# A mixture-of-experts loop: an expert's slot list made first in the program of the expert two places ahead

## The chip, the cores and the metric

The kernel runs on one core of a Trainium2 chip. The metric is the device time of one execution in microseconds (us). A core has five engines with programs of their own, which meet only at semaphores: TensorE (PE in the profile, PEld for its weight loads), VectorE (DVE), ScalarE (ACT), GpSimd (POOL) and SyncE (SP), the last of which here only starts transfers.

## The reference

The reference is a small decoder trunk in float32: 512 tokens of 1024 features, two layers. Layer 0 mixes tokens with a short gated convolution, layer 1 with sparse attention. After the mixer each layer has a mixture of 16 experts with a shared router:

```python
for e in range(N_EXPERTS):
    gate, up = jnp.split(tok @ w_gu[e], 2, axis=-1)
    out = out + comb[:, e:e + 1] * ((jax.nn.silu(gate) * up) @ w_down[e])
```

`comb` is zero except for the two experts that the router picks for a token, so an expert needs only its own tokens. `w_gu[e]` is 1024 x 1024 and `w_down[e]` is 512 x 1024, so 6 MB of weights are read for each expert. Around the mixtures stand modulation, residuals and layer norms.

## The kernel before, in words

Products are done in split form for accuracy. Every float32 operand x is written as hi + lo: ScalarE copies it to a rounded hi, VectorE subtracts to get lo, and TensorE does three matmuls (lo·hi, hi·lo, hi·hi; `mm3`, lines 203 to 205) where one would do. Weights come in blocks of 1 MB (128 x 2048 float32). For each block SyncE starts the load (`load_part`, line 916), ScalarE writes `w_hi` (`step_hi`, line 934), VectorE writes `w_lo` (`step_lo`, line 941), and TensorE does 12 matmuls of 128x512. There are six raw buffers, in which `w_lo` overwrites the raw block, and three of `w_hi`. TensorE counts used blocks in the semaphore `blk_used`, and `step_hi` of block b waits until block b - 3 is used:

```python
act.wait_ge(blk_used, b - NSPLIT + 1)        # line 938, NSPLIT = 3
```

An expert has six blocks. In the program of expert e (`expert_pe`, line 961), TensorE does blocks 0 and 1 (the second half of its own gate and up product), blocks 2 and 3 (the first half of expert e + 1's), and blocks 4 and 5 (e's `w_down`). Between block 0 and block 1 it transposes the gathered token rows of expert e + 1 (`rows_pe`, line 879, eight transposes into banks 6 and 7). ScalarE and VectorE turn these into `xe_hi` and `xe_lo` (`rows_act`, `rows_dve`). After block 2 TensorE makes the slot list of expert e + 2 and then transposes `hh`, the silu(gate)·up of expert e, which VectorE makes from ScalarE's `sg` (lines 999 and 1027).

The slot list says which token sits in which of an expert's 128 slots. Three steps make it:

- `one_hot` (line 850), VectorE: compares slot numbers with the tokens' positions, into `oneh`, of which there are two buffers. It is the first instruction of VectorE's program for expert e, for expert e + 2.
- `list_pe` (line 857), TensorE: four bf16 matmuls with two columns of output into bank 7. It waits for the one-hot (`oh_made`) and until the list before it was read (`tok_made`).
- `list_dve` (line 866), VectorE: adds the two columns into `tok`.

GpSimd waits for `tok` and starts an indirect transfer (`gather`, line 871) that fetches the 128 token rows to `xg`, two buffers. Its rows are used one program later, by `rows_pe` in the program of expert e + 1.

The order on each engine is written out by hand and is fixed. Before VectorE comes to the program of an expert it has made `w_lo` of that expert's blocks 0, 1 and 2, in the tail of the program before (line 1035, i from 5 to 8); ScalarE has made their `w_hi` in the same way (line 1005). Programs of two experts, with p = 0 and 1, form a pair; the first pair and the last are unrolled and the six between are a loop (`all_experts`, line 1052). The last pair's programs make no list.

Of the kernel before, what the change touches and what calls it, by code (L numbers as in the profile page):

```python
# [49 lines left out]
def hybrid_trunk(nc, x, c, ada_w, ada_b, ln_g, ln_b, conv_w_in, conv_w, conv_b, conv_w_out,  # L50
# [27 lines left out]
    with ExitStack() as ctx:  # L78
# [122 lines left out]
        def mm3(o, lh, ll, rh, rl, start, stop):  # L201

            nc.tensor.matmul(o, lh, rl, start=start, stop=False)  # L203
            nc.tensor.matmul(o, ll, rh, start=False, stop=False)  # L204
            return nc.tensor.matmul(o, lh, rh, start=False, stop=stop)  # L205
# [438 lines left out]
        PAIRS = NE // 2  # L644
# [75 lines left out]
        def bc(ap, shape, axis):  # L720

            return ap.unsqueeze(axis).to_broadcast(shape)
# [121 lines left out]
        def after(eng, semaphore, value):  # L844
            if not isinstance(value, int) or value > 0:
                if isinstance(semaphore, Count):
                    semaphore, value = semaphore.at(value)
                eng.wait_ge(semaphore, value)

        def one_hot(dve, s, pair, p):  # L850

            after(dve, s.tok_mm, 2 * pair + p - 1)
            shape = [P, TT, P]
            nc.vector.tensor_tensor(oneh[:, p, :, :], bc(slots[:], shape, 1),
                                    bc(posm[:, 2 * pair + p, :], shape, 2), ALU.is_equal).then_inc(s.oh_made.sem, 1)

        def list_pe(pe, s, pair, p):

            pe.wait_ge(*s.oh_made.at(2 * pair + p + 1))
            after(pe, s.tok_made, 2 * pair + p)  # L860
            for i in range(TT):
                m = nc.tensor.matmul(bank[7][:, 0:2], oneh[:, p, i, :], tokc[:, i, :], start=(i == 0),
                                     stop=(i == TT - 1))
            m.then_inc(s.tok_mm.sem, 1)

        def list_dve(dve, s, pair, p):
            dve.wait_ge(*s.tok_mm.at(2 * pair + p + 1))
            after(dve, s.xg_in[p], 16 * pair)
            nc.vector.tensor_scalar(tok[:, p, :], bank[7][:, 0:1], bank[7][:, 1:2], None, ALU.add).then_inc(s.tok_made.sem, 1)  # L869
# [6 lines left out]
                                    in_offset=bass.IndirectOffsetOnAxis(ap=tok[:, p, :], axis=0)  # L876
                                    ).then_inc(s.xg_in[p].sem, 16)

        def rows_pe(pe, s, pair, p):

            pe.wait_ge(*s.xg_in[p].at(16 * pair + 16))
            after(pe, s.xe_lo_made, 2 * pair + p)
            after(pe, s.ht_lo_made, 2 * pair + p - 1)
            pe.wait_ge(*s.tok_made.at(2 * pair + p + 1))
            for k in range(KD):
                m = nc.tensor.transpose(bank[6 + k // 4][:, (k % 4) * P:(k % 4 + 1) * P],  # L886
                                        xg[:, p, k * P:(k + 1) * P], ident[:])
            m.then_inc(s.xg_turned.sem, 1)
# [10 lines left out]
        def rows_dve(dve, s, pair, p):  # L899
            dve.wait_ge(*s.xe_hi_made.at(2 * pair + p + 1))  # L900
            for h in range(2):
                m = nc.vector.tensor_tensor(xe_lo[:, p, 4 * h:4 * h + 4, :],  # L902
                                            bank[6 + h][:].rearrange("p (k t) -> p k t", k=4),
                                            xe_hi[:, p, 4 * h:4 * h + 4, :].bitcast(F32), ALU.subtract)
            m.then_inc(s.xe_lo_made.sem, 1)
# [4 lines left out]
        def step_block(s, pair, p, i):  # L910

            first = s.b0 + 2 + EBLK * p + i
            return (first + 2 * EBLK * pair, first % NRAW, first // NRAW + 2 * EBLK // NRAW * pair,
                    first % NSPLIT)
# [26 lines left out]
        def step_lo(dve, s, pair, p, i):  # L941
            b, slot, _, hslot = step_block(s, pair, p, i)
            if not isinstance(b, int) or b < B_END:
                dve.wait_ge(hi_done, b + 1)
                nc.vector.tensor_tensor(w_lo[:, slot, :], raw[:, slot, :], w_hi[:, hslot, :].bitcast(F32),  # L945
                                        ALU.subtract).then_inc(lo_done, 1)

        def gate_up(pe, s, pair, p, i, q, j):

            b, slot, _, hslot = step_block(s, pair, p, i)  # L950
            pe.wait_ge(lo_done, b + 1)
            for kk in range(2):
                k = 2 * j + kk
                for h in range(2):
                    c_ = slice(kk * D + h * FF, kk * D + (h + 1) * FF)
                    m = mm3(bank[2 * q + h][:], xe_hi[:, q, k, :], xe_lo[:, q, k, :], w_hi[:, hslot, c_],
                            w_lo[:, slot, c_], start=(k == 0), stop=(k == KD - 1))
            m.then_inc(blk_used, 1)


        def expert_pe(pe, s, pair, p, last=False):
            e, q = 2 * pair + p, 1 - p
            gate_up(pe, s, pair, p, 0, p, 2)
            if not last:
                rows_pe(pe, s, pair + p, q)
            gate_up(pe, s, pair, p, 1, p, 3)
            if not last:
                pe.wait_ge(*s.xe_lo_made.at(e + 2))
                after(pe, s.h_made, e)
                gate_up(pe, s, pair, p, 2, q, 0)  # L970
            if not (isinstance(pair, int) and pair == PAIRS - 1):
                list_pe(pe, s, pair + 1, p)
            pe.wait_ge(*s.h_made.at(e + 1))
            for k in range(4):
                m = nc.tensor.transpose(bank[6][:, k * P:(k + 1) * P], hh[:, k * P:(k + 1) * P], ident[:])
            m.then_inc(s.h_turned.sem, 1)
            if not last:
                gate_up(pe, s, pair, p, 3, q, 1)
            pe.wait_ge(*s.ht_lo_made.at(e + 1))
            after(pe, s.y_made, e)  # L980
            for j in range(2):
                b, slot, _, hslot = step_block(s, pair, p, j + (2 if last else 4))
                pe.wait_ge(lo_done, b + 1)
                for kk in range(2):
                    k = 2 * j + kk
                    for h in range(2):
                        c_ = slice(kk * D + h * BANK, kk * D + (h + 1) * BANK)
                        m = mm3(bank[4 + h][:], ht_hi[:, k, :], ht_lo[:, k, :], w_hi[:, hslot, c_], w_lo[:, slot, c_],
                                start=(k == 0), stop=(k == 3))
                m.then_inc(blk_used, 1)  # L990
# [27 lines left out]
        def expert_dve(dve, s, pair, p, last=False):  # L1018
            e = 2 * pair + p
            if not (isinstance(pair, int) and pair == PAIRS - 1):  # L1020
                one_hot(dve, s, pair + 1, p)
            if not last:
                rows_dve(dve, s, pair + p, 1 - p)
            step_lo(dve, s, pair, p, 3)
            dve.wait_ge(*s.sg_made.at(e + 1))
            after(dve, s.h_turned, e)
            nc.vector.tensor_tensor(hh[:], sg[:], bank[2 * p + 1][:], ALU.mult).then_inc(s.h_made.sem, 1)  # L1027
            if not last:
                step_lo(dve, s, pair, p, 4)
            dve.wait_ge(*s.ht_hi_made.at(e + 1))  # L1030
            nc.vector.tensor_tensor(ht_lo[:], bank[6][:].rearrange("p (k t) -> p k t", k=4),  # L1031
                                    ht_hi[:].bitcast(F32), ALU.subtract).then_inc(s.ht_lo_made.sem, 1)
            if not (isinstance(pair, int) and pair == PAIRS - 1):
                list_dve(dve, s, pair + 1, p)
            for i in range(5, 9) if not last else range(4, 7):
                step_lo(dve, s, pair, p, i)


        def begin_pe(pe, s):
            pe.wait_ge(*s.xe_lo_made.at(1))  # L1040
            gate_up(pe, s, 0, 0, -2, 0, 0)
            gate_up(pe, s, 0, 0, -1, 0, 1)
# [200 lines left out]
        def moe_dve(dve, s):  # L1243
# [15 lines left out]
            rows_dve(dve, s, 0, 0)  # L1259
            begin_dve(dve, s)  # L1260
            all_experts(dve, expert_dve, s)
            over_dve(dve, s)
            for i in range(TT + 1):
# [19 lines left out]
        def moe_pe(pe, s):  # L1283
            for i in range(TT):
                turn_pe(pe, s.turn, us[:, i % 2, :], i)
            router_pe(pe, s)
            places_pe(pe, s)
            list_pe(pe, s, 0, 0)
            list_pe(pe, s, 0, 1)
            pe.wait_ge(*s.turn.lo.at(2 * TT))  # L1290
            pe.wait_ge(*s.tok_made.at(2))
            rows_pe(pe, s, 0, 0)
            begin_pe(pe, s)
            all_experts(pe, expert_pe, s)
            over_pe(pe, s)
# [873 lines left out]
```

## Time and profile before

| | |
|---|---|
| median of 3 runs | 1640.94 us (1638.69 to 1645.2) |
| profiled execution, its own time | 1636.06 us |
| its span, first to last instruction | 1634.3 us |
| TensorE / VectorE / ScalarE / GpSimd busy | 1293.1 / 1111.3 / 761.9 / 188.4 us |
| granted TensorE clock, mean | 0.888 |
| experts of layer 0 / of layer 1 | about 355 to 671 us / 1270 to 1579 us |

Times inside the trace count from the start of the span. "Busy" adds up the instructions' durations; matmuls overlap, so their starts tell more than their durations. The granted clock is 1.00 at 2.4 GHz and 0.50 at 1.2 GHz. In the timeline, a bracket behind an instruction gives how long its engine had been idle before it and which instruction, on which engine, ended that.

### The profile page before, as it was taken

To read this page: it belongs to the slowest core of one execution; us is meant where nothing else is said; L and a number is where in the kernel's file an instruction comes from. 1 tells how busy PE (TensorE), PEld (TensorE's weight loads), DVE (VectorE), ACT (ScalarE), POOL (GpSimd) and SP (SyncE) were. 2 spreads that over 40 slices of the span, in tenths; PEclk is the share of its full clock that TensorE was granted. 3 is DMA by queue.
4 is the path that set the end of the run, shared out by engine and by line. 5 is a ranking of instruction groups with operands and counts; after the bars stand their busy time and mean duration, and the time that the engine had idled before them with its cause. 6 is when DMAs were issued, how large, how long until landed. Compare 5 with 4: busy or idle time off the path is not lost. (4 is left out here: it accounts for less than half of the span.)

```text
span 1634.3 us, 18079 instructions
## 1 busy us (share of the span) xinstructions
PE 1293.1 (79%) x6537; PEld 1025.4 (63%) x6537; DVE 1111.3 (68%) x1210; ACT 761.9 (47%) x836; POOL 188.4 (12%) x257
## 2 busy tenths in 40 slices
PE   1499968349999999339768999999933999999950
PEld 0377747137777777238766788887822777777730
DVE  5568665648889888475644556555375699898846
ACT  0223212217777777423322444446121677777732
POOL 2011110200000000120000112111030000000012
PEclk9899989569999999659957999999965999999975
DMA  8467763229999999722401222231421799999942
GB/s 304 186 233 243 247 228 118 92 79 351 380 364 389 388 392 389 274 77 80 131 5 52 91 78 91 81 120 41 161 98 69 271 381 393 390 394 387 396 180 87
DMA packets 107407, 356.01 MB, mean 218 GB/s; under 512 B 7746, under 2 KB 16062, under 8 KB 107342
## 3 DMA queue, kind: packets, MB, share of 16 engines
q1 hardware_dynamic: 82920, 268.47, 43.7%
q0 software_dynamic: 19568, 69.78, 12.3%
q10 hardware_dynamic: 4854, 16.88, 2.5%
q8 instruction: 42, 0.69, 0.2%
q14 instruction: 23, 0.19, 0.0%
HBM read 329.89 MB, written 25.21 MB: 217 GB/s over the span
## 5 line engine op out<-in xcount | busy, mean ns | idle before, releaser
L945 DVE TENSOR_TENSOR w_lo<-raw,w_hi 128x2048 fp32r<-128x2048 f32 x189 | 433.4, 2298 | 86.9 <-ACT w_hi L939 86.8
L939 ACT ACTIVATE w_hi<-raw 128x2048 fp32r<-128x2048 f32 x189 | 362.4, 1918 | 89.5 <-PE bank L205 74.5
L203 PE MATMUL bank<-w_lo,xe_hi 128*128 128x512 f32 x512 | 212.8, 416 | 7.6 <-DVE xe_lo L902 7.3
L204 PE MATMUL bank<-w_hi,xe_lo 128*128 128x512 f32 x512 | 204.6, 400 | 0.0
L205 PE MATMUL bank<-w_hi,xe_hi 128*128 128x512 f32 x512 | 204.3, 399 | 0.0
L198 DVE TENSOR_TENSOR w_lo<-raw,w_hi 128x2048 fp32r<-128x2048 f32 x37 | 84.9, 2300 | 150.1 <-ACT w_hi L193 149.6
L193 ACT ACTIVATE w_hi<-raw 128x2048 fp32r<-128x2048 f32 x37 | 70.4, 1908 | 155.0 <-PE bank L205 154.3
L203 PE MATMUL bank<-u_lo,w_hi 128*128 128x512 f32 x320 | 134.1, 419 | 7.0 <-DVE q L1619 3.6
L205 PE MATMUL bank<-u_hi,w_hi 128*128 128x512 f32 x320 | 128.9, 403 | 0.0
L204 PE MATMUL bank<-u_hi,w_lo 128*128 128x512 f32 x320 | 128.8, 403 | 0.0
L318 DVE SCALAR_TENSOR_TENSOR acc<-ada,silu_c,acc 128x1024 f32<-128x1024 f32 x88 | 112.4, 1277 | 12.4 <-DMA ada<-in_ada_w_dram 7.7
L203 PEld LDWEIGHTS bank<-w_lo,xe_hi 128*128 128x128 f32 x512 | 97.7, 191 | 36.9 <-issue 10.8
L1855 ACT ACTIVATE prob<-bank,snm 128x512 f32<-128x512 f32 (+3 forms) x128 | 62.3, 525 | 117.2 <-DVE snm L1914 94.1
L205 PEld LDWEIGHTS bank<-w_hi,xe_hi 128*128 128x128 f32 x512 | 97.7, 191 | 23.7
L204 PEld LDWEIGHTS bank<-w_hi,xe_lo 128*128 128x128 f32 x512 | 98.0, 191 | 19.4
L203 PE MATMUL bank<-w_lo,ht_hi 128*128 128x512 f32 x256 | 103.5, 404 | 4.9 <-DVE ht_lo L1031 4.2
L358 PE MATMUL bank<-ident,us 128*128 128x128 f32 x128 | 30.4, 416 | 95.1 <-DVE us L389 95.1
L875 POOL DMA_INDIRECT xg<-scratch_u,tok x32 | 33.8, 1055 | 604.9 <-DVE tok L869 604.3
L204 PE MATMUL bank<-w_hi,ht_lo 128*128 128x512 f32 x256 | 102.5, 401 | 0.0
L205 PE MATMUL bank<-w_hi,ht_hi 128*128 128x512 f32 x256 | 102.4, 400 | 0.0
L1914 DVE TENSOR_REDUCE snm<-bank 128x1 f32<-128x384 f32 (+1 forms) x96 | 46.2, 509 | 64.3 <-PE bank L1708 64.1
L358 PEld LDWEIGHTS bank<-ident,us 128*128 128x128 f32 x128 | 24.4, 218 | 102.5 <-DVE us L389 77.5
(255 smaller groups left out, 2439.1 us busy)
## 6 DMA issues: line engine op xcount, KB each, us to landing
raw<-in_w_gu_dram SPq DMA_DIRECT2D x128, 1024.0 KB, 7.9
raw<-in_w_down_dram SPq DMA_DIRECT2D x64, 1024.0 KB, 8.3
ada<-in_ada_w_dram POOLq DMA_DIRECT2D x64, 512.0 KB, 5.6
scratch_y<-ye ACTq DMA_DIRECT2D x32, 512.0 KB, 7.4
ada<-in_ada_w_dram SPq DMA_DIRECT2D x32, 512.0 KB, 3.7
raw<-in_conv_w_in_dram SPq DMA_DIRECT2D x12, 1024.0 KB, 10.2
rows<-scratch_mods POOLq DMA_DIRECT2D x12, 512.0 KB, 5.0
raw<-in_w_kv_dram SPq DMA_DIRECT2D x6, 1024.0 KB, 9.1
```

The source lines that it names most:

```text
L193: nc.scalar.activation(w_hi[:, b % NSPLIT, :], raw[:, b % NRAW, :], ACT.Copy).then_inc(hi_done, 1)
L198: nc.vector.tensor_tensor(w_lo[:, s, :], raw[:, s, :], w_hi[:, b % NSPLIT, :].bitcast(F32), ALU.subtract).then_inc(lo_done, 1)
L203: nc.tensor.matmul(o, lh, rl, start=start, stop=False)
L204: nc.tensor.matmul(o, ll, rh, start=False, stop=False)
L205: return nc.tensor.matmul(o, lh, rh, start=False, stop=stop)
L318: nc.vector.scalar_tensor_tensor(out=a, in0=s.ring[:, t % s.n_ring, :], scalar=silu_c[:, k:k + 1], in1=a if k or s.bias is None else s.bia ...
L358: t = nc.tensor.transpose(bank[4 + n % 4][:, q * P:(q + 1) * P], src[:, (4 * h + q) * P:(4 * h + q + 1) * P], ident[:])
L875: pool.indirect_dma_start(out=xg[:, p, :], out_offset=None, in_=s.u[:, :], in_offset=bass.IndirectOffsetOnAxis(ap=tok[:, p, :], axis=0)).t ...
L939: nc.scalar.activation(w_hi[:, hslot, :], raw[:, slot, :], ACT.Copy).then_inc(hi_done, 1)
L945: nc.vector.tensor_tensor(w_lo[:, slot, :], raw[:, slot, :], w_hi[:, hslot, :].bitcast(F32), ALU.subtract).then_inc(lo_done, 1)
L1855: m = nc.scalar.activation(prob[:, n % 3, c0:c0 + w], bank[u % 3][:, c0:c0 + w], ACT.Exp, bias=snm[:, u % 3, q:q + 1])
L1914: m = nc.vector.tensor_reduce(snm[:, u % 3, q:q + 1], o[:, c0:c0 + (i + 1) * P], AX_X, ALU.max, negate=True)
```

## The change

`list_pe` moves from behind block 2 to the very start of TensorE's program for an expert, in front of block 0. `list_dve` moves from behind `ht_lo` to right behind `one_hot` in VectorE's program. As the list is now written to bank 7 before `rows_pe` writes there, `rows_pe` waits for one more read of a list (`next_listed`).

```diff
-        def rows_pe(pe, s, pair, p):
+        def rows_pe(pe, s, pair, p, next_listed):
...
-            pe.wait_ge(*s.tok_made.at(2 * pair + p + 1))
+            pe.wait_ge(*s.tok_made.at(2 * pair + p + 1 + next_listed))
...
         def expert_pe(pe, s, pair, p, last=False):
             e, q = 2 * pair + p, 1 - p
+            more = not (isinstance(pair, int) and pair == PAIRS - 1)
+            if more:
+                list_pe(pe, s, pair + 1, p)
             gate_up(pe, s, pair, p, 0, p, 2)
             if not last:
-                rows_pe(pe, s, pair + p, q)
+                rows_pe(pe, s, pair + p, q, more)
             gate_up(pe, s, pair, p, 1, p, 3)
             if not last:
                 pe.wait_ge(*s.xe_lo_made.at(e + 2))
                 after(pe, s.h_made, e)
                 gate_up(pe, s, pair, p, 2, q, 0)
-            if not (isinstance(pair, int) and pair == PAIRS - 1):
-                list_pe(pe, s, pair + 1, p)
             pe.wait_ge(*s.h_made.at(e + 1))
...
             if not (isinstance(pair, int) and pair == PAIRS - 1):
                 one_hot(dve, s, pair + 1, p)
+                list_dve(dve, s, pair + 1, p)
             if not last:
                 rows_dve(dve, s, pair + p, 1 - p)
...
-            if not (isinstance(pair, int) and pair == PAIRS - 1):
-                list_dve(dve, s, pair + 1, p)
             for i in range(5, 9) if not last else range(4, 7):
                 step_lo(dve, s, pair, p, i)
...
-            rows_pe(pe, s, 0, 0)
+            rows_pe(pe, s, 0, 0, True)
```

## Rows read from the trace of the kernel before

**Rows 1.** The page's part 1: busy us (share of the span) xinstructions.

```profile
PE 1293.1 (79%) x6537; PEld 1025.4 (63%) x6537; DVE 1111.3 (68%) x1210; ACT 761.9 (47%) x836; POOL 188.4 (12%) x257
```

**Rows 2.** Windows view, inside layer 1's experts: busy, then clock, DMA share, GB/s.

```profile
core 0: us, PE busy (x) PEld busy (x) DVE busy (x) ACT busy (x) POOL busy (x), PEclk, DMA share, GB/s
...
1300.00:1400.00 100.00, 99.08 (x474) 78.55 (x472) 90.26 (x66) 76.80 (x65) 4.69 (x5) 1.00 1.00 387
```

**Rows 3.** Timeline, one expert's start: start us, us, engine, line, operation.

```profile
499.64 0.40 PE L203 MATMUL bank<-w_lo,xe_hi 128*128 128x512 f32 x1
...
499.84 1.92 ACT L939 ACTIVATE w_hi<-raw 128x2048 fp32r<-128x2048 f32 x1 [0.88 <-PE bank L205]
...
501.79 2.29 DVE L945 TENSOR_TENSOR w_lo<-raw,w_hi 128x2048 fp32r<-128x2048 f32 x1 [0.51 <-ACT w_hi L939]
...
502.44 1.04 PE L886 MATMUL bank<-ident,xg 128*128 128x128 f32 x8
...
504.00 0.69 DVE L854 TENSOR_TENSOR oneh<-slots,posm 128x512 bf16<-128x512 f32 x1
```

**Rows 4.** Timeline, the same expert, up to the read of its list.

```profile
504.58 1.92 ACT L939 ACTIVATE w_hi<-raw 128x2048 fp32r<-128x2048 f32 x1
...
506.53 2.29 DVE L945 TENSOR_TENSOR w_lo<-raw,w_hi 128x2048 fp32r<-128x2048 f32 x1 [0.51 <-ACT w_hi L939]
...
508.73 0.68 DVE L1027 TENSOR_TENSOR hh<-sg,bank 128x512 f32<-128x512 f32 x1
...
509.04 0.25 PE L862 MATMUL bank<-tokc,oneh 128*128 128x2 bf16 x4
...
509.47 0.66 PE L975 MATMUL bank<-ident,hh 128*128 128x128 f32 x4 [0.18 <-DVE hh L1027]
...
512.13 0.22 DVE L869 TENSOR_SCALAR tok<-bank 128x1 uint32<-128x1 f32 x1
```

**Rows 5.** Timeline, the start of the next expert.

```profile
518.36 0.40 PE L203 MATMUL bank<-w_lo,xe_hi 128*128 128x512 f32 x1
...
518.56 1.92 ACT L939 ACTIVATE w_hi<-raw 128x2048 fp32r<-128x2048 f32 x1 [0.88 <-PE bank L205]
...
521.16 1.04 PE L886 MATMUL bank<-ident,xg 128*128 128x128 f32 x8
...
522.72 0.68 DVE L854 TENSOR_TENSOR oneh<-slots,posm 128x512 bf16<-128x512 f32 x1
```

**Rows 6.** Lines 862 and 875 by source; waits of TensorE in 360:650 (total, times, longest).

```profile
  DVE oneh L854: 25.5, 6
...
DMA to landing us min/median/max: 4.1/7.8/9.3
...
PE bank L203 <- DVE xe_lo L902: 2.3, 2, 2.1
...
PE bank L886 <- DMA xg<-scratch_u,tok: 1.0, 1, 1.0
```

**Rows 7.** Windows and timeline of TensorE behind its short stops.

```profile
446.40:448.50 2.10, 0.01 (x1) 0.02 (x1) 1.63 (x3) 2.10 (x3) 0.00 (x0) 1.00 1.02 396
448.60:451.90 3.30, 3.30 (x8) 2.62 (x9) 3.03 (x3) 2.52 (x3) 0.00 (x0) 0.50 1.00 410
...
660.30:666.90 6.60, 4.48 (x12) 3.41 (x13) 3.63 (x4) 2.40 (x2) 0.00 (x0) 0.50 0.72 280
...
1568.20:1574.80 6.60, 5.08 (x13) 3.85 (x14) 0.74 (x2) 0.60 (x1) 0.00 (x0) 0.50 0.00 0
...
448.49 0.77 PE L203 MATMUL bank<-w_lo,xe_hi 128*128 128x512 f32 x1 [2.11 <-DVE xe_lo L902]
...
449.49 0.63 PE L205 MATMUL bank<-w_hi,xe_hi 128*128 128x512 f32 x1
449.91 0.63 PE L203 MATMUL bank<-w_lo,xe_hi 128*128 128x512 f32 x1
...
661.00 1.12 PE L975 MATMUL bank<-ident,hh 128*128 128x128 f32 x4 [2.99 <-DVE hh L1027]
```

## The prediction, made before the changed kernel ran

> **What bounds the kernel now.** I read the page's busy shares first: TensorE is busy 79% of the span, more than any other engine, but that is an average over stages [rows 1]. The change touches only the expert loops of the two mixture stages, so I took windows inside them next. There TensorE is busy 99.1 of 100 us at a granted clock of 1.00, VectorE 90, and the DMA share is also 1.00 [rows 2]. Two resources look full. Which one ends the waits is read from the timeline: where ScalarE makes a w_hi, its idle time ended at a TensorE instruction, not at a landing [rows 3, 5]. So the weights are there and TensorE sets the pace: one expert takes 18.72 us, from 499.64 to 518.36 [rows 3, 5]. A block of weights is 12 matmuls in 2.80 us (499.64 to 502.44), 0.233 us each [rows 3].
>
> What the reader is to see in the timeline is how tightly the engines follow one another at the start of an expert [rows 3]. At 499.64 TensorE begins block 0 of an expert, which is the moment the last matmul of the expert before was issued. w_hi has three buffers, so only then may ScalarE write the w_hi of block 2 (line 938: it waits for the block three before it, and that is the last w_down block). It starts at 499.84, VectorE's w_lo of that block at 501.79, and only behind that in VectorE's program comes the one-hot for the expert two places ahead, at 504.00, 0.69 long. TensorE doesn't care today: it is in block 0 from 499.64 to 502.44 and in the eight transposes after it, and reads the one-hot at 509.04, 4.35 us after it is made [rows 4].
>
> **The list matmuls, moved to the head of TensorE's program.** They still wait for the one-hot (line 859), whose place in VectorE's program does not move, but now nothing of TensorE's work lies between the last w_down matmul and that wait. The chain in between is all on the path: 0.20 us from TensorE's block end to ScalarE, 1.95 to VectorE's start, 2.21 to the one-hot, 0.69 for it: 504.69 - 499.64 = 5.05 us. The next expert gives 522.72 + 0.68 - 518.36 = 5.04 [rows 5]. Queued behind the waiting instruction on TensorE is everything: block 0, the row transposes, block 1, and through them ScalarE's xe_hi and VectorE's xe_lo. No engine has other work that shortens the chain, since ScalarE can't make block 2's w_hi before the last w_down block is used, and the one-hot stands behind that block's w_lo. So 5.05 us of empty TensorE in each expert that makes a list; bounds 4.9 and 5.3 (the handing-on of a semaphore).
>
> Then the four list matmuls themselves: 0.25 us busy [rows 4]. Where they stood they were free, because TensorE then waited for hh: the list starts at 509.04, hh is ready at 508.73 + 0.68 = 509.41, its transposes start at 509.47. hh hangs on a chain counted from the row transposes, ScalarE's w_hi at 504.58, w_lo at 506.53, hh at 508.73 [rows 4], and this is unchanged. So taking them out of there saves nothing. In front they cost 0.25 to 0.43 us (the busy time, and the step from 509.04 to 509.47); I take 0.30, nearer the busy time.
>
> **The read of the list on VectorE.** 0.21 us at 512.13 leaves its place behind ht_lo and comes right behind the one-hot [rows 4]. It waits for the list matmuls, a quarter of a microsecond, with rows_dve queued behind it, which waits for the row transposes 3 us later anyway. Cost 0; where it is removed the next w_lo starts at most 0.21 us sooner, into slack: bounds -0.2 and +0.1 per expert, and I take 0. The added one in rows_pe's count waits for this read, done while TensorE is in block 0 (2.8 us): 0.
>
> **The gather.** Nothing else stands between the read and the gather on GpSimd's queue, so each gather leaves more than 20 us ahead of its use instead of about 8.8 us (the read's end at 512.34 to the transposes at 521.16; landing 7.8 us in the median, 9.3 at the most) [rows 4 to 6]. What late gathers cost today is one wait of 1.0 us outside the prologue [rows 6]. A 2.1 us wait in front of block 2 of one expert of layer 0, behind late weight landings, also goes, and with it 1.6 us of slow clock worked out below: together 4.7 us of gain, bounds 0 and 6. The SyncE queue gets nothing new; its loads follow TensorE's block ends and get more time per expert, so they are not late next.
>
> **The clock.** The loop runs at 1.00, 2.4 GHz, because TensorE never stops. In three places it did stop for a few microseconds. After 2.11 us of waiting at 448.49 the granted clock was 0.50 (1.2 GHz) up to 451.9, and matmuls were 0.42 to 0.43 us apart [rows 7]. After 2.99 us at 661.00 it was 0.50 from 660.3 to 666.9, and the same near 1568 [rows 7]. The new wait is 5.05 us, longer than each of these, and it comes in every expert, so I expect the fall each time. At half clock a matmul takes 0.427 instead of 0.233, that is 0.455 of the slow stretch is lost: 3.4 us slow costs 1.55 us, 6.6 us slow costs 3.0. Both ends have been seen; I take the middle, 2.3. Hardly any of it is covered: the slow stretch lies over block 0 and the row transposes, on which the chain to hh hangs.
>
> The Trainium skill's page "TensorE: Matmul & The Clock Gate", section "HAM oscillation — how this bites in real kernels", speaks against this change: a wait that recurs before each tile throttles the array again every time, so each tile starts cold, and it prices that at the throttled time times (1 - 1.2/2.4). The rows above show single falls and agree in kind; by the page's factor of 0.5 the middle would be 2.5 us, and the time 6 us longer than mine.
>
> **The sum.** Lists are made in this way for experts 2 to 15, so 14 experts in each of two layers, 28 in all (24 in the loops, 4 in their unrolled head). In the first expert of a layer the same chain holds, since its block 2 is prepared the same way. 28 x (5.05 + 0.30 + 2.3) = 214.2; less 4.7 is 209.5. The profiled execution took 1636.06 us (span 1634.3), which gives 1845.6. The median of the runs shown is 1640.94, 4.9 above the profiled one, so I forecast 1851 us.
>
> **Rivals.** (1) The clock stays at 2.4 GHz. For it: 1.0 us of waiting in layer 0 brought no fall, and TensorE is busy before and behind the wait. Against it: 2.1 us was enough. Time: 28 x 5.35 - 4.7 = 145, so 1786. (2) The slow stretch is the long one each time, or more of the chain is stretched: 28 x 8.35 - 4.7 = 229, so 1870, and some us more if the slow clock also reaches block 1. For it: two of three falls lasted 6.6 us. (3) Not slower: the one-hot is ready when TensorE gets to it, and what remains is the earlier gather. It decides at the point where the one-hot ends before the last w_down matmul is issued. Today it ends 5.05 us after it, and both program order on VectorE and the three w_hi buffers hold it there; only if ScalarE and VectorE ran one block further ahead than line 938 lets them would it be so. It would give 1641 - 4.7 = 1636. That the change does not do what it says I hold for excluded: the matmuls of the list are plainly first in TensorE's program.
>
> **How the numbers follow.** Forecast (falls at each wait, between the two lengths) 0.80, its own range 1828 to 1872; clock holds 0.08; long stretch and more 0.08; not slower 0.02, with as much for a mixture in which only few waits are paid. The range takes in the cases with and without the clock: 1784 to 1878. A measurement of this kernel can tell about 0.5% from no change, that is 8 us. Slower by over 0.5%: 0.96; within: 0.02; faster: 0.02.
>
> **What would show it.** In the profile after: TensorE's list matmuls (line 862) idle some 5 us before each of 28, released by the one-hot, 140 us in all where it is 25.5 us over the prologues today [rows 6]; the granted clock in the loops well under 1.00, about 0.8 to 0.9, with matmuls 0.43 apart in block 0; TensorE busy about 80% there; an expert every 26.4 us; DMA share near 0.7. Gathers would no longer be waited for outside the prologue. Wrong would be: a wait at line 862 under 4 us, since then something lets the one-hot run ahead; a clock of 1.00 in the loops (rival 1); or hh's transposes no longer waiting for hh.

## The result, and the profile after

| | before | after |
|---|---|---|
| median | 1639.82 us (1631.11 to 1645.2, 4 runs) | 1842.01 us (1837.66 to 1844.87, 4 runs) |
| ratio | | 1.1236, 95% interval 1.1181 to 1.1292 |
| profiled execution, own time / span | 1636.06 / 1634.3 us | 1837.66 / 1835.9 us |
| mean granted clock over the span | 0.888 | 0.848 |

The change makes the kernel 12.4% slower; the forecast was 1851 us. The two profiled executions differ by 201.6 us. Of all the runs below, one of e7 (1756.92 us) was in a slower state of the chip; it counts in that kernel's median (1727.97 us, 1727.08 without it) and not in its ratio.

The page's part 1 of the changed kernel, which answers to [rows 1]:

```profile
PE 1359.1 (74%) x6537; PEld 1068.3 (58%) x6537; DVE 1113.5 (61%) x1210; ACT 761.2 (41%) x836; POOL 184.8 (10%) x257
```

VectorE and ScalarE do the same work in the same time. TensorE does the same instructions but is busy 66 us longer, so its matmuls took longer: those of line 203 in the expert loops last 469 ns in the mean instead of 416. The rest is empty time. The waits of TensorE over the whole span (us in total, times, longest) show where:

```profile
PE bank L862 <- DVE oneh L854: 150.9, 30, 6.0
```

Two of the 30 are the prologues' (12.0 us together). 138.9 us are left for 28 waits, 4.96 each. The 25.5 us of [rows 6] counted matmuls and weight loads together; its matmul part was those same two waits.

The timeline of the changed kernel from the end of one expert to the row transposes of the next, which answers to [rows 3 and 5]:

```profile
573.31 1.91 ACT L939 ACTIVATE w_hi<-raw 128x2048 fp32r<-128x2048 f32 x1 [0.88 <-PE bank L205]
...
575.26 2.29 DVE L945 TENSOR_TENSOR w_lo<-raw,w_hi 128x2048 fp32r<-128x2048 f32 x1 [0.50 <-ACT w_hi L939]
...
577.47 0.68 DVE L854 TENSOR_TENSOR oneh<-slots,posm 128x512 bf16<-128x512 f32 x1
578.21 0.27 PE L862 MATMUL bank<-tokc,oneh 128*128 128x2 bf16 x4 [4.93 <-DVE oneh L854]
578.33 0.77 PE L203 MATMUL bank<-w_lo,xe_hi 128*128 128x512 f32 x1
578.61 0.22 DVE L869 TENSOR_SCALAR tok<-bank 128x1 uint32<-128x1 f32 x1 [0.46 <-PE bank L862]
...
582.59 1.03 PE L886 MATMUL bank<-ident,xg 128*128 128x128 f32 x8
```

The chain is the one of [rows 3], link by link, but TensorE now stands at its end. ScalarE's w_hi starts 0.2 us after the moment at which TensorE could have issued a matmul behind the last of w_down (that one starts at 572.88, and at full clock they are 0.23 us apart), w_lo follows, then the one-hot, and only then the list. Before, block 0 and the transposes ran in that time. Block 0 takes 4.26 us here (578.33 to 582.59) where it took 2.80.

Windows of the changed kernel (busy, then granted clock, DMA share, GB/s): a wait, what comes behind it, the rest of that expert, the next wait, and behind that:

```profile
546.60:551.40 4.80, 0.00 (x0) 0.00 (x0) 4.30 (x3) 2.88 (x3) 0.00 (x0) 0.92 1.02 388
551.60:557.40 5.80, 5.80 (x19) 4.54 (x19) 0.22 (x1) 0.00 (x0) 0.94 (x1) 0.50 0.43 141
557.60:573.20 15.60, 15.32 (x70) 11.80 (x68) 12.30 (x9) 11.42 (x9) 0.00 (x0) 1.00 0.84 290
573.30:577.90 4.60, 0.00 (x0) 0.00 (x0) 4.10 (x3) 2.88 (x3) 0.00 (x0) 1.00 1.02 386
578.00:581.30 3.30, 3.09 (x11) 2.52 (x12) 0.37 (x2) 0.00 (x0) 0.94 (x1) 0.50 0.51 169
...
1450.00:1550.00 100.00, 79.32 (x333) 61.54 (x332) 63.44 (x45) 54.16 (x46) 3.75 (x4) 0.88 0.77 276
```

The clock is at half (1.2 GHz) behind each wait. The profile's record of the granted clock gives 6.8 us for the slow stretch at the first of these, the last part of the wait included, and 3.4 us at the second; of the 28 stretches 20 are of the long kind and 8 of the short. It is back at 1.00 for the rest of the expert. The last row answers to [rows 2]: TensorE busy 79 of 100 us instead of 99, clock 0.88, and DMA share 0.77. Nine experts from one list to another take 682.13 - 446.92 = 235.2 us, 26.13 each instead of some 18.9 (e3 below gives the rows for it):

```profile
446.92 0.27 PE L862 MATMUL bank<-tokc,oneh 128*128 128x2 bf16 x4 [4.93 <-DVE oneh L854]
...
682.13 0.26 PE L862 MATMUL bank<-tokc,oneh 128*128 128x2 bf16 x4 [4.93 <-DVE oneh L854]
```

### The profile page after: what moved, and what is told of

It is laid out like the page before. It is cut to its first block and busy times, and to the rows that moved or that the text cites. A ratio compares the mean times of both kernels' runs of the same rounds, so it can differ in the third digit from the quotient of the medians.

```text
span 1835.9 us, 18079 instructions
## 1 busy us (share of the span) xinstructions
PE 1359.1 (74%) x6537; PEld 1068.3 (58%) x6537; DVE 1113.5 (61%) x1210; ACT 761.2 (41%) x836; POOL 184.8 (10%) x257
## 5 line engine op out<-in xcount | busy, mean ns | idle before, releaser
L203 PE MATMUL bank<-w_lo,xe_hi 128*128 128x512 f32 x512 | 240.2, 469 | 5.2 <-DVE xe_lo L902 5.2
L204 PE MATMUL bank<-w_hi,xe_lo 128*128 128x512 f32 x512 | 226.5, 442 | 0.0
L205 PE MATMUL bank<-w_hi,xe_hi 128*128 128x512 f32 x512 | 224.9, 439 | 0.0
L902 DVE TENSOR_TENSOR xe_lo<-bank,xe_hi 128x512 fp32r<-128x512 f32 x64 | 41.3, 686 | 209.6 <-ACT xe_hi L895 209.6
L895 ACT ACTIVATE xe_hi<-bank 128x512 fp32r<-128x512 f32 x64 | 34.8, 595 | 279.8 <-PE bank L886 279.8
L203 PEld LDWEIGHTS bank<-w_lo,xe_hi 128*128 128x128 f32 x512 | 111.3, 217 | 36.4 <-issue 8.0
L205 PEld LDWEIGHTS bank<-w_hi,xe_hi 128*128 128x128 f32 x512 | 111.2, 217 | 28.4
L204 PEld LDWEIGHTS bank<-w_hi,xe_lo 128*128 128x128 f32 x512 | 112.8, 220 | 21.9
L862 PE MATMUL bank<-tokc,oneh 128*128 128x2 bf16 x128 | 8.5, 170 | 152.0 <-DVE oneh L854 150.9
```

The lines of the kernel that those rows point to most:

```text
L895: m = nc.scalar.activation(xe_hi[:, p, 4 * h:4 * h + 4, :], bank[6 + h][:].rearrange("p (k t) -> p k t", k=4), ACT.Copy)
```

## The experiments

Seven more kernels ran. The first four ran beside each other, with the kernel before at 1639.27 us; the last three likewise, with it at 1636.27 us. Each edit is against the changed kernel unless its heading or text says otherwise.

### e1: the wait alone, in the kernel before

```diff
             e, q = 2 * pair + p, 1 - p
+            if not (isinstance(pair, int) and pair == PAIRS - 1):
+                pe.wait_ge(*s.oh_made.at(2 * (pair + 1) + p + 1))
             gate_up(pe, s, pair, p, 0, p, 2)
```

> The kernel before, with one wait added: TensorE waits for the one-hot of expert e + 2 at the head of its program for expert e. The list matmuls, their read and the gather stay in the expert's middle. Theory (the loss is the wait for the one-hot, and the slow clock behind it): 28 waits of 4.9 to 5.0 us and the clock falling behind each, so nearly the whole loss, 1640 + 28 x (4.95 + 2.2) = 1840, less nothing for gathers: 1832 to 1842 us. Rival (the loss hangs on the list matmuls, their read or the gather in their new places): no change, 1640 us.

Measured: 1844.05 us, ratio 1.1253 (1.1211 to 1.1295). The waits of TensorE between 380 and 700 us:

```profile
PE bank L203 <- DVE oneh L854: 60.1, 12, 5.1
```

Block 0's first matmul (line 203) waits 5.0 us for a one-hot it doesn't read. The list matmuls, their read and the gather are where they were in the kernel before, and the whole loss is there all the same. So the loss is the wait with what it brings, and none that can be seen hangs on the places of the list, the read or the gather.

### e2: the wait filled with work

```diff
             if more:
+                for _ in range(FILL):
+                    nc.tensor.matmul(bank[2 * q][:], ones_b[:], oneh[:, q, :, :], start=True, stop=True)
                 list_pe(pe, s, pair + 1, p)
```

> The changed kernel, with 21 bf16 matmuls of 512 columns put in front of the list matmuls in each of the 28 programs, into a bank that is free there and overwritten later; their results are not used. They take about 4.5 of the 5 us in which TensorE otherwise waits for the one-hot. The wait ends at the same time, but TensorE is busy up to it. Theory (about 2.2 us of 7.4 per expert are the clock that falls in the wait): the clock stays at 1.00 in the loops and the time is 1840 less 28 x 2.2 = 62, so 1778 us (1768 to 1788). Rival (the slow matmuls behind the wait come from something else than the idle time, or cost nothing on the path): 1840 us as the changed kernel, within 8.

`FILL` is 21. Measured: 1784.48 us, ratio 1.0884 (1.0842 to 1.0925). Window and one-hot starts, nine experts apart:

```profile
420.00:620.00 200.00, 194.33 (x908) 137.95 (x906) 140.54 (x101) 119.65 (x101) 7.48 (x8) 1.00 0.86 305
...
440.26 0.68 DVE L855 TENSOR_TENSOR oneh<-slots,posm 128x512 bf16<-128x512 f32 x1
...
656.78 0.68 DVE L855 TENSOR_TENSOR oneh<-slots,posm 128x512 bf16<-128x512 f32 x1
```

The clock stays at 1.00 and an expert takes 216.5 / 9 = 24.06 us. The chain to the one-hot is as long as before, since the filler doesn't touch it, so the 2.07 us per expert that went (26.13 - 24.06) are the clock's part. The medians give the same: 1842.0 - 1784.5 = 57.5, or 2.05 per wait.

### e3: the one-hot made early

```diff
-                one_hot(dve, s, pair + 1, p)
-                list_dve(dve, s, pair + 1, p)
...
             for i in range(5, 9) if not last else range(4, 7):
+                if nxt and i == 7:
+                    one_hot(dve, s, *nxt)
+                if nxt and i == 8:
+                    list_dve(dve, s, *nxt)
                 step_lo(dve, s, pair, p, i)
```

`nxt` is the list that the next program makes. The first list's one-hot and read move to `begin_dve` in the same way, and the sixth pair is unrolled.

> The changed kernel, list matmuls still first in TensorE's program, but the one-hot is made in the tail of VectorE's program before, in front of the w_lo of block 1 (where VectorE has 0.5 us of idle time), and the list is read behind that w_lo. The loop's sixth pair of expert programs is unrolled for it. Theory (only the one-hot's lateness costs): no wait at the list matmuls beyond 0.1 us, clock 1.00, an expert in 18.7 to 18.9 us, so the time of the kernel before plus 28 x 0.15 for the list matmuls no longer covered and less the late gather: 1632 to 1646 us. Rival (an early list costs in itself, by bank 7, by the row transposes' wait for its read, or by the gather beside the weight loads): over 1660 us.

Measured: 1635.77 us (10 runs), ratio 0.9983 (0.9957 to 1.0009). The list is still first in TensorE's program. The window, and one-hot starts nine experts apart:

```profile
420.00:620.00 200.00, 197.24 (x934) 154.37 (x933) 176.66 (x128) 151.62 (x129) 13.25 (x13) 1.00 1.01 386
...
420.71 0.69 DVE L854 TENSOR_TENSOR oneh<-slots,posm 128x512 bf16<-128x512 f32 x1
...
591.52 0.69 DVE L854 TENSOR_TENSOR oneh<-slots,posm 128x512 bf16<-128x512 f32 x1
```

An expert takes 170.8 / 9 = 18.98 us. The 18.72 of [rows 3 and 5] is not the mean of the kernel before: in layer 0 its undisturbed experts take about 18.72 and 18.95 us in turn. From 504.00 [rows 3], six experts on, the one-hot starts at

```profile
617.26 0.68 DVE L854 TENSOR_TENSOR oneh<-slots,posm 128x512 bf16<-128x512 f32 x1
```

which is 113.26 / 6 = 18.88 us each. The difference of 0.10 us (0.14 in layer 1) is what the list matmuls cost when nothing covers them, if the other places of the one-hot and the read cost nothing. The other 7.1 us of the change's cost are gone with the one-hot's lateness. This version equals the kernel before within what was measured.

### e4: the one-hot half as late

The edit is against e3; `begin_dve` changes in the same way.

```diff
-                if nxt and i == 7:
-                    one_hot(dve, s, *nxt)
                 if nxt and i == 8:
+                    one_hot(dve, s, *nxt)
                     list_dve(dve, s, *nxt)
```

> As the kernel with the early one-hot, but the one-hot stands one step later: behind the w_lo of block 1 and in front of that of block 2, with the read of the list right behind it. The one-hot ends about 2.35 us after the last w_down matmul is issued (520.0 + 0.7 - 518.36), so the wait is half as long. Theory with the clock falling at each wait: 28 x (2.35 + 0.15 + 1.5 to 2.9), 1752 to 1791 us. Rival, half a wait no longer brings the clock down: 28 x 2.5 = 70, 1710 us, with the clock at 1.00 in the loops. Where only some waits bring it down, between the two.

Measured: 1721.96 us, ratio 1.052 (1.0473 to 1.0566). Waits between 380 and 690 us, and the window:

```profile
PE bank L862 <- DVE oneh L854: 28.0, 13, 2.2
...
420.00:620.00 200.00, 178.02 (x803) 137.42 (x802) 154.29 (x111) 129.76 (x110) 24.68 (x9) 0.97 0.93 335
...
497.19 0.68 DVE L854 TENSOR_TENSOR oneh<-slots,posm 128x512 bf16<-128x512 f32 x1
...
520.09 0.68 DVE L854 TENSOR_TENSOR oneh<-slots,posm 128x512 bf16<-128x512 f32 x1
...
541.31 0.68 DVE L854 TENSOR_TENSOR oneh<-slots,posm 128x512 bf16<-128x512 f32 x1
```

The wait is 2.15 us as worked out, but the clock fell behind only some waits: the record of the granted clock has 12 falls of 3.4 us behind 28 waits. So neither full case held; it is the third, between them. The one-hot starts show both prices. An expert with a fall takes 22.90 us (from 497.19) and one without 21.22 (from 520.09): 1.7 us for a fall, where 1.55 was worked out from [rows 7], and 21.22 - 18.98 = 2.24 for the wait. The medians give 86.2 us above e3, and less 12 x 1.55 this is 67.6 / 28 = 2.41 for each wait; the profiled executions alone give 80.6 us and 2.21. All are above the wait's row of 2.15, since an idle time counts from the modelled end of a matmul, some 0.17 us (0.40 less 0.23) behind the moment at which the next could have been issued.

### e5: the chain made longer

```diff
+            if twice:
+                nc.vector.tensor_tensor(hh[:].rearrange("p (i t) -> p i t", t=P), bc(slots[:], shape, 1),
+                                        bc(posm[:, 2 * pair + p, :], shape, 2), ALU.is_equal)
             nc.vector.tensor_tensor(oneh[:, p, :, :], bc(slots[:], shape, 1),
```

> The changed kernel, with a second comparison of the same size (0.68 us, its result unused) put on VectorE in front of each of the 28 one-hots of the loops. Theory (TensorE's wait is the chain last w_down block, w_hi, w_lo, one-hot): the wait at the list matmuls grows from 4.95 to 5.6 us and the time by 28 x 0.68 = 19, with the clock's part about the same: 1861 us (1855 to 1870). Rival (the wait is ended by something else that takes 5 us by chance, such as the loads or ScalarE's block end): 1842 us, no change.

Measured: 1871.42 us, ratio 1.1444 (1.1411 to 1.1476), just outside the range given. Waits between 380 and 700 us, the window, and last the same window of the changed kernel:

```profile
PE bank L865 <- DVE oneh L857: 66.5, 12, 5.6
...
420.00:620.00 200.00, 155.97 (x636) 120.09 (x637) 126.44 (x95) 100.76 (x86) 7.46 (x8) 0.86 0.75 267
...
420.00:620.00 200.00, 161.90 (x684) 125.44 (x685) 128.17 (x94) 108.23 (x92) 7.49 (x8) 0.89 0.78 279
```

The wait grew by 0.6 us as forecast, so TensorE does stand at the end of that chain. 29 us were added and not 19. The clock is the difference: 0.86 instead of 0.89 in the same window of the changed kernel. By the clock's record each of the 28 slow stretches is now the long one (6.8 us), where in the changed kernel 8 of 28 were 3.4 us. The expectation of "about the same" for the clock was the miss.

### e6: the wait filled by half

The same edit as e2 with 10 matmuls instead of 21.

> As the kernel with the filled wait, but 10 matmuls of 512 columns, some 2.2 us, and then 2.8 us of idle time in front of the list matmuls. The wait ends at the same time. Between the filled wait (1784 us, clock 1.00) and the changed kernel (1842, the clock down behind each wait). Theory, the clock goes by how long TensorE stands still: the wait halved by an earlier one-hot (2.1 to 2.2 us still) brought the clock down behind 12 of 28 waits, for 3.4 us each; 2.8 us still should do so behind more, 18 to 28 of 28 for 3.4 us or more each, 1.5 us lost each time: 1811 to 1830 us. Rival, a wait with work in it never lets the clock fall: 1784 us.

Measured: 1817.0 us, ratio 1.1097 (1.1056 to 1.1138). Waits between 380 and 700 us, and the window:

```profile
PE bank L863 <- DVE oneh L855: 36.0, 13, 2.8
...
420.00:620.00 200.00, 177.31 (x772) 131.14 (x778) 133.35 (x94) 114.18 (x96) 7.46 (x8) 0.94 0.81 287
```

2.77 us of standing still in each expert: 21 falls behind 28 waits, 3.4 us each. The time above e2, 32.5 us, is 1.55 us for each of the 21, the price worked out for a short fall from [rows 7].

### e7: the list behind block 0

```diff
-            if more:
-                list_pe(pe, s, pair + 1, p)
             gate_up(pe, s, pair, p, 0, p, 2)
+            if more:
+                list_pe(pe, s, pair + 1, p)
```

> The changed kernel with the list matmuls behind block 0 and in front of the row transposes, so that the 2.8 us of block 0 cover a part of the chain to the one-hot. Theory: the wait is 5.0 - 2.8 = 2.2 us in each of 28 programs, as long as with the half-late one-hot but in another place; 28 x (2.2 + 0.2) = 67 and about 12 to 28 falls of the clock at 1.5 us: 1724 to 1750 us. Rival (what counts is that the list stands ahead of the row transposes, whose wait for its read is then on the path in full, or that the wait stretches the chain to hh a second time): over 1780 us.

Measured: 1727.97 us, ratio 1.0561 (1.0524 to 1.0599). Waits of TensorE between 380 and 700 us:

```profile
PE bank L862 <- DVE oneh L854: 27.9, 13, 2.2
PE bank L886 <- DVE tok L869: 5.3, 13, 0.4
```

One block of cover takes 2.8 us off the wait, and what is left is as long as e4's and costs about as much; the clock fell behind 15 of 28 waits, behind two of them for 6.8 us. The second row is the wait that the change added to `rows_pe`: with block 0 no longer between the list and the row transposes it is on the path, 0.41 us each. In the changed kernel it costs nothing.

## Why the prediction was right, point by point

| term, per expert | forecast | layer 0 | layer 1 | from |
|---|---|---|---|---|
| wait for the one-hot | 5.05 | 5.08 | 5.15 | e2's expert less e3's: 24.06 - 18.98; 24.06 - 18.91 |
| list matmuls uncovered | 0.30 | 0.10 | 0.14 | e3's expert less the kernel before's: 18.98 - 18.88; 18.91 - 18.77 |
| slow clock behind the wait | 2.3 | 2.07 | 2.12 | the changed kernel's expert less e2's: 26.13 - 24.06; 26.18 - 24.06 |
| sum | 7.65 | 7.25 | 7.41 | |

The experts of layer 1 are means of 12, from the starts of the list matmuls. 14 x (7.25 + 7.41) = 205.2, and the profiled executions differ by 201.6. That leaves a gain of 3.6 us elsewhere, where 4.7 was forecast.

- **What bounds the loop.** TensorE's program sets the pace, and what is put on it is paid in full (e1, e5). The DMA share of 1.00 did not set the pace, but it left little room: in the kernel before 13 of the w_hi of line 939 waited for a landing, by up to 2.3 us, so "the weights are there" held for most blocks and not for all. With the longer experts the share fell to 0.77 and no w_hi waited for a landing. Whether the loads would bound a faster loop was not tried.
- **The wait.** The step from "the one-hot ends 5.05 us behind the last w_down matmul" to "TensorE stands still that long" held to 0.1 us, and e1 shows that it needs nothing of the rest of the change. That the three w_hi buffers (line 938) hold the chain back was read from the code and the rows; a kernel with four was not tried. That program order on VectorE is the other half is shown by e3 and e4.
- **The list and its read.** The list was forecast at 0.30 and cost 0.10 to 0.14, half or less. e1 and the changed kernel agree within their intervals, so it can't be seen in the total. That an expert of the kernel before takes 18.72 us was a reading of the shorter of two lengths; the sum does not use it, but the "26.4" for an expert after does (26.13 measured).
- **The gather.** The landing's median went from 7.8 to 4.3 us, and no gather was waited for outside the prologue. The time from the first expert's transposes of hh to the last's tells the gain apart: in the kernel before it is 288.3 us in layer 0 and 280.9 in layer 1, in the changed kernel 377.1 and 377.5. What made layer 0 the longer one, the gather's wait and the 2.1 us stop among it, is gone. But the forecast gave this to the earlier gather, and that is not shown: in e1, where the gathers leave as late as before, none is waited for outside the prologues either, the 2.1 us stop is gone too, and the layers take 378.0 and 377.4 us. The longer expert is enough for it. The earlier gather may be too: in e3, with experts as short as before, no gather is waited for outside the prologues and the layers take 284.7 and 283.7 us.
- **The clock.** That it falls behind every wait held (28 of 28), and e2 shows that the idle time is the cause. The size was 0.2 us too high, and the forecast's way to it, the middle between a short and a long stretch, came near by two errors that cancel in part. 20 of 28 stretches were long ones, which at 0.455 would give 2.66 us in the mean; but a part of most passes while TensorE still waits and costs nothing (the window 546.60:551.40 above has a clock of 0.92 with TensorE idle). Three experts of the changed kernel in a row show it by their one-hots, with 577.47 above between the first two of these:

```profile
550.76 0.68 DVE L854 TENSOR_TENSOR oneh<-slots,posm 128x512 bf16<-128x512 f32 x1
...
602.94 0.68 DVE L854 TENSOR_TENSOR oneh<-slots,posm 128x512 bf16<-128x512 f32 x1
...
629.19 0.69 DVE L854 TENSOR_TENSOR oneh<-slots,posm 128x512 bf16<-128x512 f32 x1
```

They take 26.71, 25.47 and 26.25 us, that is 2.65, 1.41 and 2.19 above e2's 24.06, and by the clock's record the slow stretch reached 6.0, 3.2 and 5.0 us past the start of the list: about 0.44 us lost for each us of slow matmuls. The Trainium skill's page "TensorE: Matmul & The Clock Gate", section "HAM oscillation — how this bites in real kernels", was borne out in kind: a wait that recurs brings a cold start each time. The 2.5 us estimated by its factor of 0.5 are further from 2.07 than the rows' 2.3.
- **The rivals.** The clock staying up gave 1786 us; e2, in which it does stay up, measured 1784. Not slower: its point of decision, the one-hot ready when TensorE comes to it, is what e3 makes true. Its 1636 us is e3's 1635.77, but that says little: the interval of e3's ratio (0.9957 to 1.0009) also holds no difference at all.

## What to carry to other kernels

Moving an operation first in one engine's program moves its wait too: before doing it, look up when its input is made on the other engine, counted from the last instruction that will then stand in front of it. In this loop each engine's next step hangs on a buffer that TensorE frees at its block ends, so an operation behind such a step in program order is late by the whole chain (here 5 us), and it is hidden only as long as TensorE has enough to do first: one block, 2.8 us, left 2.2 us of the wait (e7). TensorE standing still for 5 us in each expert cost about four tenths more than the stop itself, as the clock fell with it (2.07 to 5.08). Filling that wait with unused matmuls gave 58 of the 202 us back; making the input earlier gave all of it back (e3).

## What the runs showed of the hardware that was not expected

**The clock and short stops.** A stop of 2.15 us in every expert brought the clock to half behind 12 of 28 stops (e4), the same length in another place behind 15 of 28 (e7), 2.77 us behind 21 of 28 (e6), 4.96 us behind 28 of 28. So a stop of 2 to 3 us here was neither safe nor certain to cost the clock, and 0.6 us more of waiting (e5) cost another 0.45 us per expert through longer slow stretches ((29.4 - 28 x 0.6) / 28).

**The indirect transfer beside VectorE.** The gather's issue on GpSimd takes 0.94 us in most cases and 2.74 us where a w_lo had begun 0.35 us before it, as throughout e4 (its timeline):

```profile
477.24 2.28 DVE L945 TENSOR_TENSOR w_lo<-raw,w_hi 128x2048 fp32r<-128x2048 f32 x1
477.59 2.74 POOL L875 DMA_INDIRECT xg<-scratch_u,tok  x1 [20.14 <-DVE tok L869]
```

In e3 it begins 0.1 us ahead of the w_lo and takes 0.94 (timeline of e3):

```profile
1467.19 0.94 POOL L875 DMA_INDIRECT xg<-scratch_u,tok  x1 [17.99 <-DVE tok L869]
1467.29 2.30 DVE L945 TENSOR_TENSOR w_lo<-raw,w_hi 128x2048 fp32r<-128x2048 f32 x1 [0.37 <-ACT w_hi L939]
```

The kernel before has one such case in each layer, and the one in layer 0, behind a w_lo of 376.38, is the gather that was waited for in [rows 6]. In its other experts the w_lo begins only 0.01 to 0.03 us ahead, and the issue takes 0.94 (its timeline; the first row is two w_lo merged):

```profile
376.73 2.74 POOL L875 DMA_INDIRECT xg<-scratch_u,tok  x1 [28.20 <-DVE tok L869]
...
512.60 4.60 DVE L945 TENSOR_TENSOR w_lo<-raw,w_hi 128x2048 fp32r<-128x2048 f32 x2 [0.25 <-ACT w_hi L939]
...
512.62 0.94 POOL L875 DMA_INDIRECT xg<-scratch_u,tok  x1 [17.78 <-DVE tok L869]
```

Here the wait was hidden in e4, as the gather has a whole expert's time to land. The Trainium skill's page "SBUF — State Buffer", section "SBUF: two separate sides", says that VectorE and GpSimd share a port pair, that a VectorE instruction with two inputs in SBUF (as w_lo has) needs it against a GpSimd instruction that reads SBUF, and that whoever starts first holds it for its whole instruction. The 2.74 us agree with that, if the issue reads its offsets `tok` from SBUF at its start: 477.59 plus 2.74 is 0.8 us behind the end of the w_lo at 479.52, which is about the 0.94 us of an undisturbed issue. The other direction does not agree: in e3 the gather was first, and the w_lo behind it took 2.30 us and was not held up for the 0.94. No run here tells why a lead of 0.02 us did not delay the gather.
